# A gated feed-forward by seven quarter products, in parts of 8, 8 and 6 tiles

## The reference

```
def swiglu_ffn(x, w_in, w_down):
    a, b = jnp.split(x @ w_in, 2, axis=-1)
    return (jax.nn.silu(a) * b) @ w_down

x = x + 0.5 * swiglu_ffn(rmsnorm(x, ffn1_norm), ffn1_w_in, ffn1_w_down)
u = rmsnorm(x, mix_norm)
proj = u @ w_in                    # queries, keys, values, gates, state-space input
...                                # state space, attention, memory attention, merge
x = x + 0.5 * swiglu_ffn(rmsnorm(x, ffn2_norm), ffn2_w_in, ffn2_w_down)
```

## Time and profile before

| | |
|---|---|
| median of 3 runs | 2407.32 us |
| the profiled execution | 2408.05 us, span 2406.2 us |
| TensorE busy, share of the chain that ended last | 2387.4 us (99%), 91% |
| VectorE, ScalarE, GpSimd busy | 66%, 45%, 14% |
| granted TensorE clock, mean | 0.999 of full speed |
| memory traffic | 107 GB/s over the span |

### The profile page before, as it was taken

How to read it: one execution, slowest core, us unless ns; L and a number is a source line. 1 busy time by engine, 2 the same in 40 slices (tenths; PEclk the granted TensorE clock), 3 DMA queues, 4 the chain that set the end, 5 groups by cost and what they waited for, 6 DMA issues and landing times.

```text
span 2406.2 us, 33984 instructions
## 1 busy us (share of the span) xinstructions
PE 2387.4 (99%) x13482; PEld 2014.7 (84%) x13482; DVE 1589.6 (66%) x2231; ACT 1094.5 (45%) x1626; POOL 339.6 (14%) x259
## 2 busy tenths in 40 slices
PE   9999999999999999999999999999999999999998
PEld 7877988998886889889988888877778788889997
DVE  7775775665977577556644347769995386359685
ACT  5346553554445546346523236522235564335444
POOL 1231030001132120001111124300000121120001
PEclk9999999999999999999999999999999999999999
DMA  4312222322230222223222235643442143222322
GB/s 169 145 45 84 92 79 97 123 88 106 100 129 18 106 89 104 88 105 107 87 105 88 104 103 183 223 144 118 145 148 89 42 171 133 93 105 79 115 87 88
DMA packets 46849, 260.13 MB, mean 108 GB/s; under 512 B 5424, under 2 KB 7984, under 8 KB 22768
## 3 DMA queue, kind: packets, MB, share of 16 engines
q1 hardware_dynamic: 44448, 249.07, 29.3%
q0 software_dynamic: 640, 5.51, 0.6%
q10 hardware_dynamic: 1616, 3.54, 0.5%
HBM read 240.27 MB, written 16.78 MB: 107 GB/s over the span
## 4 chain that ended last, share of the span: by engine, by line
PE 91%; DVE 5%; ACT 2%; issue 2%; DMA 0%; DVEq 0%; SPq 0%; ACTq 0%
PE gemm L487 60%; PE gemm L1104 5%; PE gemm L1105 5%; PE gemm L1106 5%; PE gemm L780 1%; PE gemm L791 1%; PE gemm L782 1%; DVE w_lo L437 1%; DVE out_sb L1909 1%; PE turned L1418 1%; PE mixed L1432 1%; PE score L1409 1%; ACT w_hi L429 1%; PE gemm L674 1%; PE gemm L673 1%
## 5 line engine op out<-in xcount | busy, mean ns | idle before, releaser
L437 DVE TENSOR_TENSOR w_lo<-w_raw,w_hi 128x2048 fp32r<-128x2048 f32 (+4 forms) x157 | 341.8, 2177 | 206.7 <-ACT w_hi L429 206.6
L487 PE MATMUL gemm<-h_hi,w_hi 128*128 128x512 f32 x1136 | 454.4, 400 | 2.4 <-DVE w_lo L437 1.9
L487 PE MATMUL gemm<-h_hi,w_lo 128*128 128x512 f32 x1136 | 443.3, 390 | 0.0
L487 PE MATMUL gemm<-h_lo,w_hi 128*128 128x512 f32 x1136 | 442.7, 390 | 0.0
L429 ACT ACTIVATE w_hi<-w_raw 128x2048 fp32r<-128x2048 f32 (+4 forms) x167 | 293.0, 1754 | 186.2 <-PE gemm L487 169.1
L487 PEld LDWEIGHTS gemm<-h_hi,w_hi 128*128 128x128 f32 x1136 | 213.6, 188 | 57.6 <-issue 9.1
L487 PEld LDWEIGHTS gemm<-h_hi,w_lo 128*128 128x128 f32 x1136 | 213.2, 188 | 45.7
L487 PEld LDWEIGHTS gemm<-h_lo,w_hi 128*128 128x128 f32 x1136 | 213.7, 188 | 42.1 <-issue 1.0
L487 PE MATMUL gemm<-f_hi,w_hi 128*128 128x512 f32 x480 | 187.3, 390 | 0.6
L487 PE MATMUL gemm<-f_hi,w_lo 128*128 128x512 f32 x480 | 186.8, 389 | 0.0
L487 PE MATMUL gemm<-f_lo,w_hi 128*128 128x512 f32 x480 | 186.7, 389 | 0.0
(11 more groups left out here) (549 smaller groups left out, 5287.9 us busy)
## 6 DMA issues: line engine op xcount, KB each, us to landing
w_raw<-in_w SPq DMA_DIRECT2D x179, 1024.0 KB, 4.8
w_raw<-in_w SPq DMA_DIRECT2D x12, 768.0 KB, 4.3
w_raw<-in_w SPq DMA_DIRECT2D x17, 512.0 KB, 3.8
trig_kept<-made SPq DMA_DIRECT2D x16, 512.0 KB, 6.0
trig<-trig_kept SPq DMA_DIRECT2D x16, 512.0 KB, 6.7
w_raw<-in_w SPq DMA_DIRECT2D x8, 640.0 KB, 4.6
bias_t<-in_att_bias SPq DMA_DIRECT2D x2, 1536.0 KB, 8.8
decay_t<-in_c_decay SPq DMA_DIRECT2D x2, 1536.0 KB, 8.1
```

Of the source, the lines that this page charges most:

```text
L437: dve.tensor_tensor(flat(w_lo, b), flat(w_raw, b), flat(w_hi, b).bitcast(F32), ALU.subtract).then_inc(S["w_rest"], 1)
L487: mm = pe.matmul(dst, lhs, rhs, start=b.first and k == 0 and j == 0, stop=b.last and k == b.kt - 1 and j == 2)
```

## The change

ffn1 takes the form of ffn2. The plan of weight blocks is made by one function for both:

```diff
+    def gated(name):
+        for part, tiles in enumerate(GATED_PARTS):
+            start[f"{name}_up{part}"] = len(out)
+            at = sum(GATED_PARTS[:part])
+            if part:
+                for t in range(at, at + tiles):
+                    out.append(Piece(0, t * P, WCOLS, KD, "seven", name + "_in"))
+            else:
+                for j in range(tiles // 2):
+                    for c in (0, F2):
+                        out.append(Piece(0, c + j * WCOLS, WCOLS, KD, "feat", name + "_in"))
+            start[f"{name}_down{part}"] = len(out)
+            for j in range(DM // WCOLS):
+                out.append(Piece(at * P, j * WCOLS, WCOLS, tiles, "feat", name + "_down"))
```

The functions of ffn2 for an up run, its down blocks and its gate (`seven_part`, `down_rounds`, `down_rests`, `up_gated`) become common to both, with the same order inside, and take the name and the part. Loops over up blocks are written out. Placement of the side work:

```diff
+        WAVES_AT = {(0, 1): (0,), (0, 2): (1,), (0, 3): (2, 3), (1, 0): (4, 5, 6), (1, 1): (7, 8, 9),
+                    (1, 2): (10, 11, 12), (1, 3): (13, 14, 15)}
...
+            def wave_kept(s):                                  # on ScalarE
+                act.wait_ge(S["trig_s"], 3 * s + 3)
+                act.dma_start(trig_kept[s], made[s % 3][:]).then_inc(S[f"trig_moved{s % 3}"], 16)
...
+            for part in range(len(GATED_PARTS)):               # ScalarE
+                ups, downs = gated_blocks("ffn1", part)
+                if part:
+                    seven_part("ffn1", part)
+                for j, b in enumerate(downs):
+                    down_rounds("ffn1", part, j)
+                    if (part, j) == (0, 1):
...
+                    for s in WAVES_AT.get((part, j), ()):
+                        waves(s)
+                        wave_kept(s)
+                    if (part, j) == (LAST_PART, 0):
+                        log_and_exp(act)
+                        act.wait_ge(S["mem_in"], 16)
+                        norm_squares(act, mem_sb, mem_t)
+                    if (part, j) == (LAST_PART, 1):
+                        norm_rooted(act, N0 + 1, MEM)
+                    if (part, j) == (LAST_PART, 2):
+                        split_hi(act, J0 + 1, mem_t, S["normed"], cnt("normed", 0), hi=m_hi)
+                    if part == LAST_PART and j >= 2:
+                        norm_squares(act, x_sb, x2_sq, wait=(S["g_free"], downs[0].t0),
+                                     tiles=range(0, 4) if j == 2 else range(4, 6))
...
+            for part in range(len(GATED_PARTS)):               # VectorE
+                if part:
+                    seven_part("ffn1", part)
+                for j in range(DM // WCOLS):
+                    if (part, j) == (LAST_PART, 1):
+                        mem_squares_added()
+                    if (part, j) == (LAST_PART, 2):
+                        mem_scaled()
+                    down_rests("ffn1", part, j)
+                    if (part, j) == (LAST_PART, 3):
+                        add_square(dve, N0 + 2, KD - 2, x2_sq)
+                    if (part, j) == (0, 0):
+                        steps_and_turns()
+                    for s in WAVES_AT.get((part, j), ()):
+                        for step_at in range(3):
+                            phase_step(s, step_at)
...
+                    def mem_total(m):                          # TensorE, in the middle of a tile
+                        if (part, j, m) == (LAST_PART, 1, 1):
+                            pe.wait_ge(S["sq_added"], added_by(MEM_NORM))
...
             silu_by_root(0, 2)                                 # GpSimd
+            pool.wait_ge(S["units"], plan2[AT2["ffn1_down0"]].u0)
             pool.dma_start(time_t[:], A["c_time"]).then_inc(S["time_in"], 16)
+            token_sums(pool, gated_counts("ffn1"))
...
             for s in range(STILES):
                 whole_turns(s)
+            pool.wait_ge(S["units"], plan2[AT2[f"ffn1_down{LAST_PART}"]].u0)
+            pool.dma_start(mem_sb[:], A["mem"].rearrange("(k p) t -> p k t", p=P)).then_inc(S["mem_in"], 16)
             squares_added(pool, N0 + 2, x2_sq, KD - 2)
```

More of the change, by code:

```diff
@@ L209, in third_pieces @@
     out, start = [], {}
[L211 to L223, removed]
+    def gated(name):
[12 more added lines that the diff above has]
+                out.append(Piece(at * P, j * WCOLS, WCOLS, tiles, "feat", name + "_down"))
+    gated("ffn1")
     start["mk"] = len(out)
@@ L254, in third_pieces @@
         out.append(Piece(0, c, WCOLS, KD, "feat", "w_out2"))
[L255 to L267, removed]
+    gated("ffn2")
     return out, start
@@ L2481, in third_tensor, with seven_part @@
-            ffn("ffn1", 0, N0, sq_f, cnt("h_ready", 0))
+            def seven_part(name, part):
+                ups, downs = gated_blocks(name, part)
+                if part == 1:
+                    pe.wait_ge(S["whole"], gated_counts(name)("whole", KD + 4))
+                for b in ups:
+                    seven(pe, b)
+                pe.wait_ge(S["first_out"], 2 * ups[-1].count + 2)
+                pe.wait_ge(S["seven_out"], 4 * ups[-1].count + 4)
+            ups, downs = gated_blocks("ffn1", 0)
@@ new lines, in third_tensor @@
+            opening_in_halves(pe, ups[:2], 2 * DEPTH - 1, sq_f)
+            for n, b in enumerate(ups[2:]):
+                product(pe, b, h_hi, h_lo, each=None if n else second_total(pe, 2 * DEPTH - 1, sq_f))
+            for part in range(len(GATED_PARTS)):
[6 more added lines that the diff above has]
+                            pe.wait_ge(S["sq_added"], added_by(MEM_NORM))
+                            pe.matmul(o_ps[:, 0:MEM], ones[:], mem_t[:, 0, :], start=True,
+                                      stop=True).then_inc(S["norm_sum"], 1)
+                    product(pe, b, g2_hi, g2_lo, tile_ready=None if j else (S["g2_s"], sum(GATED_PARTS[:part])),
+                            halfway=mem_total)
@@ L2695, in third_tensor @@
             for part in range(len(GATED_PARTS)):
[L2696 removed]
                 if part:
[L2698 to L2703 removed]
+                    seven_part("ffn2", part)
+                ups, downs = gated_blocks("ffn2", part)
                 for j, b in enumerate(downs):
@@ new lines, in seven_part @@
+            def seven_part(name, part):
+                ups, downs = gated_blocks(name, part)
+                for u, b in enumerate(ups):
+                    if u:
+                        pair_round(act, b, 3)
+                    one_product(act, b)
+                    if u:
+                        gated_round(ups[u - 1], u - 1)
+                    for q in range(3):
+                        if q == 2:
+                            gate_kept(b)
+                        if not b.closes:
+                            pair_round(act, plan[b.n + 1], q)
+                        elif q < 2:
+                            begun_round(act, downs[0], q)
+                    gate_silu(b)
+                gated_round(ups[-1], len(ups) - 1)
+                round_block(act, downs[1].n)
@@ L2938, in third_scalar @@
+            norm_squares(act, x_sb, x2_sq, wait=(S["g_free"], downs[0].t0), tiles=(KD - 2, KD - 1))
             norm_rooted(act, N0 + 2)
@@ L3231, in third_scalar @@
+                if part < LAST_PART:
+                    for j, b in enumerate(downs):
+                        down_rounds("ffn2", part, j)
             log_and_exp(act)
```

568 lines of the change are left out of this document (224 added, 344 removed).

## The result

The changed kernel takes 2448.16 us (median of 4, 2447.96 to 2448.93), the kernel before 2407.36 on the same chips: a ratio of 1.017, 95% interval 1.0158 to 1.0182. It is slower by 40.8 us; the forecast was 2437, slower by 29.7, with 2426 to 2442 as its own range and 2417 to 2450 as the whole one. So the time lies 6 us above the range of the mechanism that was forecast, and inside the whole one.

A forecast was written before the change was run, and what follows sets the result against it. TensorE, busy 99% of the span, was taken to bound the kernel, so added waits land in full: -11.3 + 16.4 + 16.3 + 7.7 = +29.1 us, median 2407.32 to 2436.4, taken as 2437, range 2417 to 2450.

The forecast's parts named there:

- The gain: Feed-forward up blocks: 14 converted tiles, seven quarter products each instead of 48 wide matmuls, save TensorE 11.3 us.
- First edge: Opening of part 1's seven-product blocks: waves 0 to 3 queued ahead delay ScalarE's first copy; 16.4 us, bounds 6.5 and 20.
- the forecast's 6.9: Part 0's token rounding: wave 0 end to end, 6.4 us, plus about 0.5 for ScalarE's write issue, slides everything behind.
- Second edge: Opening of part 2's seven-product blocks: waves 4 to 15, three per down block, delay the copy; 16.3 us, bounds 8.7 and 24.
- the ring: Part 1's down blocks: three wave buffers cycle through turns, VectorE, ScalarE, issue and landing; 12.8 us per three waves against 10.88.
- Rival (d): Part 1's down blocks: buffer cycle slower than priced as weights share queues with writes; edge 24 us, total 2445; chance 0.10.
- Memory's norm and the end: Last part's down blocks, memory products and mixing projection: waits for norm total, first key block and squares; 7.7 us, bounds 4 and 12.
- The 0.8 for the mixing projection: Start of the mixing projection: it begins with weight rests behind the late squares' total, costing 0.8 us.
- Clock: TensorE behind the long waits: forecast adds nothing for a lower clock; bounds nothing or +6 us.
- rival (c): Behind each long TensorE wait: losses as forecast, and the clock falls too; 2443 us, chance 0.20.
- Rival (b): Both openings and the end: lag absorbed, only work after the down blocks counts, +8 us; 2415, chance 0.16.
- Rival (a): Whole changed feed-forward: waves hidden, only the 11.3 us saving left; 2396 us, chance 0.04.

The follow-up runs named there:

- filled run: Changed kernel with matmuls into an unused bank at seven places where TensorE waits; 2445.59 us, ratio 1.0157.
- last kernel: Changed kernel with waves respread over up and down blocks, memory's norm taken apart, its squares ahead of part 2's first down-block rounding; 2402.97 us, ratio 0.9981.
- run with early steps: Changed kernel with the waves' coefficient rows made on VectorE behind part 0's third up block, not beside GpSimd's token sums; 2446.39 us, ratio 1.0158.
- early-wave run: Changed kernel with coefficient rows made early, eleven waves behind part 0's fourth to eighth up blocks, five in part 1's first two down blocks; 2426.39 us, ratio 1.0079.

## Why the prediction was right, and by how much it was not

**The gain** of 11.3 us is confirmed at 11.5 by the sums above; it is a remainder, so it holds whatever else changed elsewhere in the kernel.

**First edge**, forecast 16.4, measured 20.1. The mechanism is as told: wave 0 ahead of the token rounding, waves 1 to 3 ahead of the copy. Step by step: the first product at E+5.9 (forecast E+4.4); the copy done and the fifth product begun at E+22.1 (E+20.0); what comes behind the fifth product 3.7 us (2.2). Wave 0 pushed the token rounding back by 10.2 us (1288.58 to 1298.80) and not 6.9; that the sums had ended 1.9 us earlier than assumed hid half of it. The 3.3 us more come from three places: GpSimd's turns waited 1.6 for the small coefficient steps; VectorE took the wave up 1.2 after its turns were done (1292.41), behind two additions and a weight rest; and its steps beside GpSimd take 1.17 + 0.98 + 0.58 instead of 0.75 + 0.75 + 0.43:

```profile
1281.23 2.37 DVE L3242 TENSOR_TENSOR state_par<-par_sb,state_par 128x16 f32<-128x16 f32 x1
1283.63 0.18 DVE L3243 TENSOR_TENSOR state_par<-par_sb,state_par 128x16 f32<-128x16 f32 x1
...
1293.60 1.17 DVE L3263 SCALAR_TENSOR_TENSOR made<-time_t,state_par,made 128x512 f32<-128x512 f32 x1
```

Moving the coefficient steps gave back 0.9 of it. The 6.3 that is left without the waves' work looks like the forecast's 6.9 and does not bear it out: VectorE's steps and ScalarE's activations, more than half of the 6.9, are gone there, and the clears are new.

**Second edge**, forecast 16.3, measured 18.5. The copy starts at 1470.57 and the fifth product at 1471.10, E+21.8 with E = 1449.28 (forecast E+19.9), and 2.4 comes behind (2.2). But the ring was the wrong mechanism. The writes land in 2.6 us, not 6.0 (DMA issues, 1290 to 1480 us: count, KB each, median us to landing); the issue takes 0.33, and ScalarE goes on 0.40 us behind the last activation, near the 0.5 of the forecast:

```profile
trig_kept<-made ACTq DMA_DIRECT2D x16, 512.0 KB, 2.6
```

Yet the first write of each down block stands where the forecast had it, 1425.03 = E-24.3 and then every 13 to 14 us (forecast 12.8). Between the first two of these rows stand wave 7's last turn, a rounding, a rest and wave 7's first step:

```profile
1425.03 0.33 ACTq L2855 DMA_DIRECT2D trig_kept<-made  x1
...
1428.47 1.49 POOL L2761 TENSOR_SCALAR made<-made 128x512 f32<-128x512 f32 x1
...
1430.08 1.92 ACT L419 ACTIVATE w_hi<-w_raw 128x2048 fp32r<-128x2048 f32 x1 [0.46 <-ACT made L2850]
...
1432.04 2.29 DVE L427 TENSOR_TENSOR w_lo<-w_raw,w_hi 128x2048 fp32r<-128x2048 f32 x1 [3.63 <-ACT w_hi L419]
1434.24 1.18 DVE L3263 SCALAR_TENSOR_TENSOR made<-time_t,state_par,made 128x512 f32<-128x512 f32 x1
...
1439.04 0.33 ACTq L2855 DMA_DIRECT2D trig_kept<-made  x1
...
1452.54 0.33 ACTq L2855 DMA_DIRECT2D trig_kept<-made  x1
...
1465.59 0.33 ACTq L2855 DMA_DIRECT2D trig_kept<-made  x1
```

What sets this pace is ScalarE and VectorE waiting for each other in turn. ScalarE's rounding of the next weights stands behind two more waves (1430.08), VectorE's rest waits 3.63 us for that rounding, wave 7's steps stand behind the rest (1434.24), and ScalarE's next wave waits for the steps. Wave 7's turns had been done since 1429.96, and those of waves 10 and 13 were done 2.1 and 3.4 us before VectorE took them up, so in these rounds VectorE waits neither for GpSimd nor for a landing. The step of the prediction that failed here is the ring through the landing; a round of the chain that took its place lasts 13.0 to 14.0 us, near the 12.8, and that is luck. Rival (d), a slower ring, falls with the ring.

**Memory's norm and the end**, forecast 7.7 over the kernel before; measured C + D = 13.8, on the same footing, since D is counted from the kernel before with the 0.44 us that it lost there. This is the step that was mis-sized most. Its waits were as said, a little longer (1.84 for 1.6, 3.73 for 3.2, 3.50 for 2.7). What is missing are the matmuls behind them at half rate, 4.8 us: the bound on the clock was drawn for the two openings alone. The filled run gives 3.1 of it back; the rest stood ahead of the wait for the squares' total and only shortened that. The 0.8 for the mixing projection shows in no row of TensorE's waits.

**Clock**, forecast 0 with bounds 0 and +6, a rival at 2443. The fall came, after 1.84 us of waiting as after 10.8. The Trainium skill's rule cited in the prediction ("TensorE: Matmul & The Clock Gate", "What's actually happening"), that the clock falls with idleness and comes back with work, agrees with these rows. Its price was neither forecast: 12 us of matmuls over their pitch, 3 of them on the path. The prediction's own test for rival (c), slow matmuls behind the waits, was met, and the rival was still not the cause; slow work is a price only where nothing else is later. Of the 11.9 us by which the sum of 52.3 exceeds the forecast's losses of 40.4, 3.7 are the first edge's, 2.2 the second's, 6.1 the end's. Rival (b), lag absorbed, is answered by A and B themselves, 20.1 and 18.5 against its 6.5 and 8.7. Rival (a), waves hidden and 2396, is not the changed kernel, but it is what the form allows: the last kernel, with no wave's cost at either edge, stands 7 us above it, 5.7 of them at memory's norm and the end.

Not settled: no run takes VectorE's steps away alone or changes the order of rounding, rest and waves within a block, so the chain of the second edge is read from the trace and not tried; and how much of the 3.7 us behind the fifth product is VectorE's missing lead.

## What to carry to other kernels

When side work moves to another stage, ask not whether its engine has idle time there but what stands behind it in that engine's queue, and when that is wanted: the same sixteen waves' work costs almost nothing (A + B = 0.1, U = 1.2 in the last run) or 33 us by its place. Price each place by itself (a table of lateness by stretch does it in one run each) before choosing a spread. Slow matmuls behind a wait are a price only if nothing later in the block was late anyway. And a total that comes out near its forecast does not show the mechanism: the second edge was 2.2 us off with a ring that was not there.

## What was not expected of the hardware

The first of twelve VectorE instructions on 128x16 elements took 2.37 us, the second 0.18, beside GpSimd's 11.8 us of sums (rows above); two more took 2.39 and 2.25. In the run with early steps, away from the sums, each of the twelve took 0.16 to 0.18. Writes of 512 KB on ScalarE's queue landed in 2.6 us at the median, where on SyncE's queue, behind the weights, it was 6.0; the queue and the traffic around it changed together, so no run here tells which made the difference. Behind the wait of 1.84 us the first matmuls still started 0.23 us apart; then, from 1545.99 to 1549.37, eight of them started 0.43 apart, at a granted clock of 0.50. And no table load stands between silu and sine in the up blocks of the early-wave run (1205 to 1287 us), so alternating them cost nothing there.
